# Two neighbouring weight pieces split by one operation of 2048 columns instead of two of 1024

## The reference

```
h = rms_norm(x)
proj = h @ w_in                     # 2048 x 10240: HGRN2 q,f,i,g | S5 u | stick-breaking q,k,v | 3 gates
o_a = HGRN2 recurrence(...)         # gated linear recurrence
o_b = S5 complex diagonal scan, GLU # (gelu(y) @ w_glu)
o_c = stick-breaking attention(...)
merged = sum_k sigmoid(gate_k) * (o_k @ w_branch[k])
x = x + merged @ w_out              # 2048 x 2048
h2 = rms_norm(x)
up = causal_depthwise_conv(h2 @ w_up)   # 2048 x 11264, width 3
x = x + (silu(up[:D_FF]) * up[D_FF:]) @ w_down
```

## Time and profile before

| | |
|---|---|
| median of three runs | 1488.71 us (1488.54 to 1490.02) |
| profiled execution, first to last instruction (its span) | 1487.2 us |
| TensorE matmul busy | 1420.0 us, 95% |
| VectorE busy | 1091.9 us, 73% |
| ScalarE busy | 773.8 us, 52% |
| GpSimd busy | 433.7 us, 29% |
| w_lo, L834, 500 instructions | 638.7 us |
| w_hi, L559, 500 instructions | 511.9 us |
| load of one 512 KB piece of w_up, issue to landing (median) | 3.3 us |

### The profile page before, as it was taken

The page is one execution under the profiler, slowest core; times in us unless marked ns, Lnnn a source line. Parts: engine busy times, 40 slices in busy tenths (PEclk is TensorE's granted clock), DMA queues, the critical chain, the costliest instruction groups (busy, mean ns, idle before and its releaser), DMA issues.

```text
span 1487.2 us, 24696 instructions
## 1 busy us (share of the span) xinstructions
PE 1420.0 (95%) x8128; PEld 1240.5 (83%) x8128; DVE 1091.9 (73%) x1370; ACT 773.8 (52%) x1098; POOL 433.7 (29%) x385
## 2 busy tenths in 40 slices
PE   5999999998787899989999999999999999999999
PEld 4889988886676788768888888888888888888887
DVE  5897758889999857776768877777777776554543
ACT  5564457674444456544555555555555555433442
POOL 5044411254876723982211111111111110000000
PEclk9999999999999999999999999999999999999999
DMA  7554544553343545455546555555555556666663
GB/s 215 172 184 160 167 162 150 170 171 115 126 142 127 182 156 201 156 166 185 187 169 211 185 187 193 186 191 188 190 190 183 195 187 185 189 202 207 184 206 111
DMA packets 74339, 261.45 MB, mean 176 GB/s; under 512 B 8560, under 2 KB 9104, under 8 KB 74160
## 3 DMA queue, kind: packets, MB, share of 16 engines
q1 hardware_dynamic: 73152, 256.41, 53.3%
q0 software_dynamic: 992, 4.37, 0.8%
q10 hardware_dynamic: 144, 0.01, 0.0%
HBM read 258.66 MB, written 2.10 MB: 175 GB/s over the span
## 4 chain that ended last, share of the span: by engine, by line
PE 74%; DVE 14%; POOL 5%; issue 3%; ACT 2%; DMA 1%; SPq 0%; DVEq 0%; POOLq 0%; ACTq 0%
PE bank L295 47%; PE bank L297 25%; DVE w_lo L834 5%; DVE tmp L842 3%; PE pair L316 2%; DVE tmp L1085 2%; POOL gated L1354 2%; POOL proj L1262 2%; DVE tmp L849 1%; ACT w_hi L559 1%; DMA gates<-xT 1%; POOL merged L1359 1%; POOL merged L1361 1%; DVE gated L839 0%; DVE gates L839 0%
## 5 line engine op out<-in xcount | busy, mean ns | idle before, releaser
L834 DVE TENSOR_TENSOR w_lo<-raw,w_hi 128x1024 fp32r<-128x1024 f32 x500 | 638.7, 1287 | 311.8 <-ACT w_hi L559 307.7
L559 ACT ACTIVATE w_hi<-raw 128x1024 fp32r<-128x1024 f32 x500 | 511.9, 1029 | 409.8 <-PE bank L297 377.6
L295 PE MATMUL bank<-a_in,w_hi 128*128 128x512 f32 x1536 | 554.5, 402 | 47.3 <-DVE w_lo L834 40.1
L295 PE MATMUL bank<-h,w_hi 128*128 128x512 f32 x1408 | 488.4, 390 | 0.0
L297 PE MATMUL bank<-a_in,w_lo 128*128 128x256 f32 x1536 | 439.1, 286 | 0.0
L297 PE MATMUL bank<-h,w_lo 128*128 128x256 f32 x1408 | 397.1, 282 | 0.0
L295 PEld LDWEIGHTS bank<-a_in,w_hi 128*128 128x128 f32 x1536 | 295.5, 192 | 119.5 <-issue 35.2
L295 PEld LDWEIGHTS bank<-h,w_hi 128*128 128x128 f32 x1408 | 264.4, 188 | 55.4
L297 PEld LDWEIGHTS bank<-a_in,w_lo 128*128 128x128 f32 x1536 | 297.6, 194 | 0.5 <-issue 0.5
L297 PEld LDWEIGHTS bank<-h,w_lo 128*128 128x128 f32 x1408 | 266.1, 189 | 0.0
L295 PE MATMUL bank<-act,w_hi 128*128 128x512 f32 x704 | 244.1, 390 | 0.0
(11 more groups left out here) (166 smaller groups left out, 1122.5 us busy)
## 6 DMA issues: line engine op xcount, KB each, us to landing
raw<-w_up SPq DMA_DIRECT2D x176, 512.0 KB, 3.3
raw<-w_in SPq DMA_DIRECT2D x160, 512.0 KB, 4.2
raw<-w_down SPq DMA_DIRECT2D x80, 512.0 KB, 4.4
raw<-w_out SPq DMA_DIRECT2D x32, 512.0 KB, 3.3
raw<-w_br SPq DMA_DIRECT2D x16, 512.0 KB, 3.6
raw<-w_br SPq DMA_DIRECT2D x16, 256.0 KB, 3.3
raw<-w_down SPq DMA_DIRECT2D x16, 256.0 KB, 2.7
gates<-xT SPq DMA_DIRECT2D x4, 512.0 KB, 10.2
```

The lines of the kernel that those rows point to most:

```text
L295: pe.matmul(bank[b][:, :], w[:, k * P:(k + 1) * P], a.rearrange("p a t -> p (a t)"), start=first and n == 0, stop=False, skip_group_check= ...
L559: act_e.activation(w_hi[s][:, 0:blocks * P], raw[s][:, 0:blocks * P], ACT.Copy).then_inc(hi_ready, 1)
L834: ve.tensor_tensor(w_lo[s][:, w], raw[s][:, w], w_hi[s][:, w].bitcast(F32), ALU.subtract).then_inc(lo_ready, 1)
```

## The change

The four slots of `raw`, `w_hi` and `w_lo` become slices of three tensors, so that slots 0 and 1, and slots 2 and 3, lie side by side. In the input, output and up projections the two pieces of a tile are then split by one ScalarE operation of 2048 columns (`hi_pair`) and one VectorE operation of 2048 columns (`lo_pair`). `hi_pair` waits for both loads and for `piece_used` at the second piece's value, p0+1-3, and raises `hi_ready` by 2; `lo_pair` waits for `hi_ready` p0+2 and raises `lo_ready` by 2. The first pieces of the program and those of the GLU, branch and down projections stay single, except the down projection's first four. TensorE's, GpSimd's and SyncE's code stays as it is.

```diff
-        raw = [sb(f"raw{s}", [P, PIECE * P]) for s in range(RING)]
-        w_hi = [sb(f"w_hi{s}", [P, PIECE * P], F32R) for s in range(RING)]
-        w_lo = [sb(f"w_lo{s}", [P, PIECE * P], F32R) for s in range(RING)]
+        raw_ring = sb("raw", [P, RING * PIECE * P])
+        hi_ring = sb("w_hi", [P, RING * PIECE * P], F32R)
+        lo_ring = sb("w_lo", [P, RING * PIECE * P], F32R)
+
+        def slots(ring):
+            return [ring[:, s * PIECE * P:(s + 1) * PIECE * P] for s in range(RING)]
+
+        raw, w_hi, w_lo = slots(raw_ring), slots(hi_ring), slots(lo_ring)
...
+            def hi_pair(i, per, p0):
+
+                p, s = i * per + p0, p0 % RING
+                for c in range(2):
+                    act_e.wait_ge(raw_landed[s + c], i * (16 * per // RING) + 16 * (p0 // RING + 1))
+                if not (isinstance(p, int) and p < RING):
+                    act_e.wait_ge(piece_used, p + 1 - (RING - 1))
+                w = slice(s * PIECE * P, (s + 2) * PIECE * P)
+                act_e.activation(hi_ring[:, w], raw_ring[:, w], ACT.Copy).then_inc(hi_ready, 2)
...
             for n in range(IN_TILES):
-                for p in (2 * n + 4, 2 * n + 5):
-                    hi(0, RING, p)
+                if 2 * n + 4 < GLU_P:
+                    hi_pair(0, RING, 2 * n + 4)
+                else:
+                    for p in (2 * n + 4, 2 * n + 5):
+                        hi(0, RING, p)
                 copy_half(n, n, piece_used, 2 * n + 2)
                 mixers(n + 1)
...
-                    for c in range(2):
-                        if last and j >= 2:
-                            hi(0, RING, DOWN_P + 2 * (j - 2) + c)
-                        else:
-                            hi(i, 2 * BANKS, UP_P + 2 * (j + 2) + c)
+                    if last and j >= 2:
+                        hi_pair(0, RING, DOWN_P + 2 * (j - 2))
+                    else:
+                        hi_pair(i, 2 * BANKS, UP_P + 2 * (j + 2))
...
+            def lo_pair(i, per, p0):
+
+                p, s = i * per + p0, p0 % RING
+                ve.wait_ge(hi_ready, p + 2)
+                w = slice(s * PIECE * P, (s + 2) * PIECE * P)
+                ve.tensor_tensor(lo_ring[:, w], raw_ring[:, w], hi_ring[:, w].bitcast(F32), ALU.subtract).then_inc(lo_ready, 2)
```

More of the change, by code:

```diff
@@ L752, in outs @@
                 for j in range(BANKS):
-                    for c in range(2):
-                        if last and j >= 2:
-                            hi(0, RING, UP_P + 2 * (j - 2) + c)
-                        else:
-                            hi(i, 2 * BANKS, OUT_P + 2 * (j + 2) + c)
+                    if last and j >= 2:
+                        hi_pair(0, RING, UP_P + 2 * (j - 2))
+                    else:
+                        hi_pair(i, 2 * BANKS, OUT_P + 2 * (j + 2))
                     copy_half(i * BANKS + (OUT_T + j), j, piece_used, i * (2 * BANKS) + (OUT_P + 2 * j + 2))
@@ L1120, in _ @@
             for n in range(IN_TILES):
-                for p in (2 * n + 4, 2 * n + 5):
-                    lo(0, RING, p)
+                if 2 * n + 4 < GLU_P:
+                    lo_pair(0, RING, 2 * n + 4)
+                else:
+                    for p in (2 * n + 4, 2 * n + 5):
+                        lo(0, RING, p)
                 add_halves(n, n, proj(n))
@@ L1170, in outs @@
                 for j in range(BANKS):
[L1171 to L1175, removed]
+                    if last and j >= 2:
+                        lo_pair(0, RING, UP_P + 2 * (j - 2))
+                    else:
+                        lo_pair(i, 2 * BANKS, OUT_P + 2 * (j + 2))
                     t = i * BANKS + j
@@ L1212, in ups @@
                     q = i * 2 + (j - 3) // 2
[L1213 to L1217, removed]
+                    if last and j >= 2:
+                        lo_pair(0, RING, DOWN_P + 2 * (j - 2))
+                    else:
+                        lo_pair(i, 2 * BANKS, UP_P + 2 * (j + 2))
                     if first and j == 1:
```

## The result

| | before | after |
|---|---|---|
| median of four runs | 1489.37 us | 1558.37 us (1555.52 to 1562.83) |
| span of the profiled execution | 1487.2 us | 1554.5 us |
| ratio of the runs, 95% interval | | 1.0465 [1.0445, 1.0484] |

The changed kernel is 69 us slower by the medians, 67.3 by the spans. Forecast were 1550, 1518 to 1580. In the rows of the changed kernel L857 is `lo_pair`, L574 `hi_pair`, L300 and L302 the matmuls with w_hi and w_lo, L862 `add_halves`, L792 silu, L815 act_hi, L1219 and L1221 the convolution.

A forecast was written before the change was run, and what follows sets the result against it. TensorE's matmul count was taken to bound the kernel while weights are split in time. Losses of 28 (up), 3.5 (output) and 31 us (input), 62.5 on 1487.2, gave 1549.7; adjusted to the median 1551, stated as 1550, range 1518 to 1580.

The forecast's parts named there:

- sizes, 2048 columns: Time of one two-piece split, extrapolated from smaller instructions: 1.92 us on ScalarE, 2.33 us on VectorE.
- up projection: 88 tiles: chain between ScalarE and VectorE takes 11.66 us per two tiles against TensorE's 11.08, 25 us; start 3; together 28.
- output projection: 16 tiles: 5.93 us per tile against 5.54; twelve loop tiles lose 4.7, less 1.0 of play: 3.5 us.
- first tiles: Input projection, first 13 tiles: waits that now last until the pair is done, 3 us.
- level products: Input projection, HGRN2's eight products: VectorE's factor comes 1.96 us later, so TensorE waits 1.07 each time, 8 us.
- normalisations and scores: Input projection: ScalarE returns late from waiting for a mean; with queries, keys and stick-breaking scores 9 us, bounds 3 and 15.
- S5: Input projection's S5 scan, VectorE nearly full: about 3 us for each of three table periods and 2 around them, 11 us.
- The mean's shift: Start of the up projection: second norm's mean on VectorE comes 1.96 us later, delaying the next split; 3 us once.
- the loops do not close: Rival: up and output projections lose nothing in their loops, only bursts stay: 34 us, 1523 us; chance 0.14.
- two in one cost as much as two: Rival: a merged split saves no fixed part; up projection 56 us, output 7.6, input 36: 1588 us; chance 0.06.
- a faster kernel: Rival: saved fixed parts decide; VectorE in the S5 scan saves 3.3 us over 25 tiles: 1485 us; chance 0.04.
- pairs land late: Rival: two pieces requested together share DMA engines, so input projection pairs wait too: 15 us more, 1565 us; chance 0.03.

The follow-up runs named there:

- the run with the permit alone: Kernel before, two single instructions per engine, but ScalarE's first also waits for both loads and the second slot: 1498.4 us, ratio 1.0064.

## Why the prediction was right

**The time.** 1550 forecast, 1558.4 measured. Its steps against the starts of the groups above, and within the input projection against the starts of single tiles; lateness is how much later the same tile starts than before:

| step | forecast | shown |
|---|---|---|
| sizes, 2048 columns | 1.92 and 2.33 us | 1.91 and 2.29 |
| up projection | 28 | 37.8 |
| output projection | 3.5 | 3.8 |
| first tiles | 3 | 5.9 |
| level products | 8 | 8.1 (lateness 5.9 at the first, 14.0 behind the last) |
| normalisations and scores | 9 | 6.9 (14.0 to 20.9) |
| S5 | 11 | 3.0 (20.9 to 23.9) |
| down projection | 0 | 1.8 |

**Right, and shown.** That the ScalarE and VectorE chain closes in the up projection: 11.68 and 11.99 us between silus, in turn, for a forecast of 11.62 and 11.70, against 11.09 before; and the runs that move silu turn the loss off in the one kernel and change nothing in the other. The output projection, to 0.3 us: ScalarE's h comes every 5.86 us, 5.98 in every other pair of tiles, for a forecast of 5.93.

```profile
709.25 0.51 ACT L778 ACTIVATE h<-x,gain_ffn  x1 [3.27 <-DVE x L1205]
709.67 1.90 ACT L574 ACTIVATE w_hi<-raw 128x2048 fp32r<-128x2048 f32 x1
...
715.11 0.51 ACT L778 ACTIVATE h<-x,gain_ffn  x1 [3.28 <-DVE x L1205]
```

That the price is lost overlap and not the late slot: the run with the permit alone. That a level product waits for what VectorE's 1.96 us minus 0.89 leave, 1.07: rows of 1.03 and 1.04, gone with single pieces. That eight of these make 8 us is right by luck. The first product had waited 0.88 before the change, the second waits 0.17 now, and these two cost 0.6 together; each of the other six costs 1.30, since the bracket leaves out part of the loss here too.

**Mis-sized.** The up projection, by 10 us. From the start of its fifth tile on it lost 30.6 us, where I had 25. I counted the turn of the program's loop as 0.40 in place of 0.32, and it took 0.62, which is 0.22 of the 0.32 us by which four tiles lost more than I said (1.48, not 1.16). The other terms of the chain came out 0.06 longer in two tiles (11.68 for 11.62). Up to the start of the fifth tile it lost 7.1, where I had 3. The mean's shift gave one wait, forecast at 3 us:

```profile
808.13 0.50 PE L300 MATMUL bank<-h,w_hi 128*128 128x512 f32 x1 [2.97 <-DVE w_lo L857]
```

That is the 2.97; the output projection's lateness added one of 1.91 for `h` before it, and behind this come four microseconds at a mean granted clock of 0.57, mostly at the 1.2 GHz level (0.50):

```profile
785.73 0.50 PE L300 MATMUL bank<-h,w_hi 128*128 128x512 f32 x1 [1.91 <-DVE h L1207]
```

```profile
786.00:790.00 4.00, 4.00 (x14) 3.16 (x14) 1.44 (x1) 2.18 (x2) 0.37 (x2) 0.57 0.46 182
```

That is 1.9 us and, as an estimate from 4 us at 0.57, some 1.7 us which I had not counted. In the experiment with the up projection alone the wait for `h` is absent, the long one (2.96) is there, and 3.1 us are lost up to the start of the fifth tile.

S5, by 8 us: I carried VectorE's delay through three periods and left out that GpSimd ended last there; the tiles in which TensorE comes out of a table period start at 352.6, 406.3 and 456.1 us before, 53.8 and 49.8 apart, and at 376.1, 430.6 and 482.0 now, 54.4 and 51.5 apart, so these two periods cost 0.7 and 1.7 us, not 3 each. The tile whose wait I had made 1.1 longer waits 2.48 us, beside 2.50 in the earlier trace rows:

```profile
440.40 0.47 PE L300 MATMUL bank<-a_in,w_hi 128*128 128x512 f32 x1 [2.48 <-DVE w_lo L857]
```

It starts 24.2 us later than before; of that the first branch product keeps 23.9. So the up projection came out 10 us above and S5 8 us below its forecast; the good total is partly luck. What makes a period cheaper than I walked it I have not isolated. The first tiles lost twice what I said: a tile at 80.0 waits 2.22 us for its low half where before there was no wait. The normalisations and scores lost 2 us less.

**The signs.** I expected over 100 waits for w_lo; there are 70, with the two for single pieces. I expected a wait of about 1 us before each level product; seven of the eight have it, and six of these are new. The forecast of 0.6 us once in two tiles is seen as a loss and not in the brackets. At 340 us the lateness is 20.9 to 23.6 of the 67.3, so most of the difference lies behind it, as I had said.

**The rivals.** That the loops do not close, and that two in one cost as much as two, fall with the rows above; a faster kernel falls with every run with pairs. That pairs land late was not seen: a piece of w_in lands in 4.0 us by the median (before 4.2), one of w_up in 3.8 in place of 3.3, and ScalarE's waits that the profile puts down to a load of w_in went from 12, 30.0 us, to one of 3.0. The Trainium skill's rule of a fixed cost per SBUF instruction ("VectorE: DVE Perf Modes", section "The TRN2 errata") is borne out in busy time, and decides nothing, since what ended the kernel was when the low halves were ready and not how long VectorE was busy. Two instructions of 1.225 us became one of 2.293, 0.16 us for each of 182 pairs, some 29 of the 47 us that VectorE's busy time fell; the rest must lie in the input projection, where the durations differ beside GpSimd's instructions.

## What to carry to other kernels

Before two instructions of a hand-over between engines are merged, write down the chain that leads from one engine to the other and back, with starts from the timeline, and compare its length with the bottleneck engine's for the same number of tiles: merged, the first engine's second half no longer overlaps the second engine's first half, and this is lost each time that the chain passes through the hand-over (twice in two tiles here). An operation that waits for late work and stands ahead of the feeding of the bottleneck engine belongs behind it; the move cost nothing here where the chain was short. The saved fixed parts were worth nothing here, on two engines that had idle time and whose results came late.

## What the hardware showed that was not expected

The turn of a program's loop on ScalarE has a price that differs between kernels. From act_hi to w_hi it is 0.32 us inside the loop, and over the turn 0.39 before, 0.62 in the changed kernel and 0.52 with pairs in the up projection alone. That no idle time covers it is not the reason: the kernel with single splits on ScalarE and pairs on VectorE has as little idle time there and takes 0.39. The five kernels with 0.52 or more have `hi_pair`, with its two waits for loads, at the top of the loop; why it is 0.52 in one and 0.62 in another stays open.

TensorE's short waits are understated in their brackets: 0.71 us was lost at the row that shows 0.45 and 0.58 at the one that shows 0.31, since the bracket counts from the modelled end of the matmul before, and the first matmul behind the wait takes longer. A granted clock of 1.00 stood in the window of the up projection through a wait every second tile. The length of a single wait does not tell what follows: behind the 1.91 us the clock read 0.57 over four microseconds, behind the longer 2.97 us it read 1.00 in every microsecond to 814.

In the input projection VectorE's low halves take 2.68 us in the mean where GpSimd works beside them for over half of their time, and 2.29 where it does not. No run here takes GpSimd's work away, so that it is the cause is not shown.
